# The first weights of experts 4 to 30: four loads of 2 MB for each expert, in place of two of 4 MB

## The chip, the cores and the metric

The kernel runs on one core of one Trainium2 chip. The metric is device time in microseconds (us); of several executions the median counts. A core has TensorE (PE) for matmuls, VectorE (DVE), ScalarE (ACT), GpSimd (POOL), SyncE (SP), which here does nothing but issue loads and stores, and 16 DMA engines that move data between HBM and the on-chip memory (SBUF, 128 partitions).

## The reference

One layer: two token mixers (sparse attention and retention) on 256 tokens of width 1024, and then the part that this document is about, a mixture of 32 experts of which each token uses 4. In float32 throughout:

```python
def moe_ffn(h, w_router, b_router, w1, b1, w2, b2):
    logits = (jnp.einsum('bsd,de->bse', h, w_router) + b_router).astype(jnp.float32)
    top_val, top_idx = lax.top_k(logits, TOP_K)
    ...
    for e in range(N_EXPERTS):
        z = jnp.einsum('bsd,df->bsf', h, w1[e]) + b1[e]
        glu = jnp.minimum(z[..., 0::2], SWIGLU_LIMIT)
        lin = jnp.clip(z[..., 1::2], -SWIGLU_LIMIT, SWIGLU_LIMIT)
        act = glu * jax.nn.sigmoid(SWIGLU_ALPHA * glu) * (lin + 1.0)
        out = out + combine[..., e:e + 1] * (jnp.einsum('bsf,fd->bsd', act, w2[e]) + b2[e])
    return out
```

The first weights w1[e] are 1024 x 2048 numbers (8 MB), the second weights w2[e] 1024 x 1024 (4 MB): 12 MB for an expert and 384 MB in all, every byte read once.

## The kernel before

After the mixers and the router (the first 170 us), the kernel goes through the experts in one sweep, gathering up to 64 tokens for each. On PE one expert is one `step`: eight calls of `z_rows`, each with four matmuls on one row of 2048 numbers of w1 in each partition, and in between smaller pieces (gather and transposes for the next expert, the scatter of results); at its end `down` multiplies the activations of the expert before, e - 1, with its w2, also in eight rows (`k`), four on each half of w2.

Where the weights lie: `w1r` has 16 rows of 128 x 2048 numbers (16 MB), that is room for the w1 of two experts, rows 0 to 7 for even ones and 8 to 15 for odd ones (`par`); `w2r` has room for one w2 (4 MB) in two halves. `w1_used` counts finished rows of w1, `w2_used` finished quarters of w2, both incremented by PE.

SP issues all loads of weights from one queue, in an order that is written out by hand. `load_w2(e, c)` loads half a w2, 2 MB, with runs of 16 KB in each partition. `load_w1(e, i, pair)` loads a quarter of a w1, 2 MB and two rows; it is used for experts 0 to 3 and 31. Experts 4 to 30 go by `next_half(base, e, par, h)`: SP waits until four rows are used, then loads half a w1, 4 MB and four rows, with runs of 32 KB. `next_w2(base, e)` waits for each half of w2 and loads it. `ahead(e, x, par)` is w2 of expert e and then w1 of expert x; `between` puts w2 behind the first half of w1. The loop `Fori(3, 6)` uses `between`, the loop `Fori(6, 15)` uses `ahead`. At the end come the quarters of expert 31 (`next_w1`), the w2 of expert 29 (`next_w2`), and in `last_w2` the w2 of 30 and 31, which go into freed rows of `w1r`; the last one is cut finer still.

PE waits for w1 at the first row of each part: for a half on `w1_half` at rows 0 and 4, for a quarter on `w1_in` at rows 0, 2, 4 and 6. `final` is the last step, with expert 31; the results are normalised and stored behind it.

Of the kernel before, what the change touches and what calls it, by code (L numbers as in the profile page):

```python
# [21 lines left out]
P = 128  # L22
# [7 lines left out]
TOPK_KEYS = 64  # L30
NE, TOPK, FF = 32, 4, 1024
SLOTS = 64
HALVES = 14
SWEEPS = S // SLOTS
KW = P + S
RMS_EPS, LN_EPS = 1e-5, 1e-6
# [38 lines left out]
def hybrid_block(nc, x, norm1_gain, w_in, rel_bias, idx_k_ln_gain, idx_k_ln_bias, ret_gn_gain, w_out,  # L75
# [3 lines left out]
    with ctx:  # L79
        def sb(name, shape, dt=F32):  # L80
            return ctx.enter_context(nc.sbuf_tensor(name, shape, dt))

        def sem(name):
            return ctx.enter_context(nc.semaphore(name))


        w1r = sb("w1r", [P, 16, 2048])
# [127 lines left out]
        dve_chain = sem("dve_chain")  # L215
        w1_in = [sem(f"w1_in{i}") for i in range(8)]
        w2_in = [sem(f"w2_in{i}") for i in range(2)]
        w1_half = [sem(f"w1_half{i}") for i in range(4)]
        w1_early = sem("w1_early")
        w2_last = [sem(f"w2_last{i}") for i in range(6)]  # L220
        w1_used = sem("w1_used"); w2_used = sem("w2_used")
# [11 lines left out]
        x_v = x[0].rearrange("(t p) d -> p t d", p=P)  # L233
        win_v = w_in[0].rearrange("(k p) n -> p k n", p=P)
        w1_v = w_mlp1[0].rearrange("e (c p i a) f -> e c i p (a f)", c=2, p=P, i=2)
        w1_c = w_mlp1[0].rearrange("e (c p j) f -> e c p (j f)", c=2, p=P)
        w2_v = w_mlp2[0].rearrange("e (c p j) d -> e c p (j d)", c=2, p=P)

        C_QI, C_QKB, C_VB, C_GB, C_QA, C_KA, C_VA = range(7)
# [4 lines left out]
        def _(sp):  # L244
# [51 lines left out]
            sp.wait_ge(out_mm, 4)  # L296
            load_w1(1, 0, 4)

            def next_half(base, e, par, h):
                sp.wait_ge(w1_used, 8 * base + (8 * (e - 2) + 4 * h + 4))  # L300
                at = 8 * par + 4 * h
                sp.dma_start(w1r[:, at:at + 4, :].rearrange("p a f -> p (a f)"), w1_c[e, h]).then_inc(w1_half[2 * par + h], 16)

            def next_w1(base, e, par, pairs=range(4)):
                for i in pairs:
                    sp.wait_ge(w1_used, 8 * base + (8 * (e - 2) + 2 * i + 2))
# [20 lines left out]
            def rest_of_sweep(base):  # L327

                def ahead(e, x, par):
                    next_w2(base, e)  # L330
                    next_half(base, x, par, 0)
                    next_half(base, x, par, 1)

                def between(e, x, par):
                    next_half(base, x, par, 0)
                    next_w2(base, e)
                    next_half(base, x, par, 1)

                sp.wait_ge(w1_used, 8 * base + 1)
                sp.dma_start(w1r[:, 0, :], w1_v[2, 0, 0, :, 0:2048]).then_inc(w1_early, 16)  # L340
                sp.wait_ge(w1_used, 8 * base + 2)
                sp.dma_start(w1r[:, 1, :], w1_v[2, 0, 0, :, 2048:4096]).then_inc(w1_in[0], 16)
                next_w1(base, 2, 0, range(1, 4))
                next_w1(base, 3, 1)
                ahead(1, 4, 0)
                ahead(2, 5, 1)
                ahead(3, 6, 0)
                next_w2(base, 4)
                with sp.Fori(3, 6) as m:
                    between(2 * m - 1, 2 * m + 1, 1)  # L350
                    between(2 * m, 2 * m + 2, 0)
                with sp.Fori(6, NE // 2 - 1) as m:
                    ahead(2 * m - 1, 2 * m + 1, 1)
                    ahead(2 * m, 2 * m + 2, 0)
                next_w1(base, NE - 1, 1)
                next_w2(base, NE - 3)
                last_w2(base)
# [4 lines left out]
            with sp.If(n > 1):  # L362
                with sp.Fori(1, n) as r:
                    base = sp.snap(r * NE)
# [678 lines left out]
        def _(pe):  # L1043
# [57 lines left out]
            halves = (slice(0, 64), slice(64, 128))  # L1101
# [28 lines left out]
            for which in range(2):  # L1130
                for g in range(2):
                    for t in range(TT):
                        at = 256 * which + 128 * g
# [27 lines left out]
            for b in range(2):  # L1161
                for j in range(4):
                    k, t = 2 * b + j // 2, j % 2
# [148 lines left out]
                    ins = nc.tensor.transpose(ps[:, 7, P * j:P * j + P], hg[:, P * j:P * j + P], ident)  # L1312
                ins.then_inc(hg_tr, 1)

            def z_rows(base, lap, k, par, halves, early=None):

                if halves and k % 4 == 0:
                    pe.wait_ge(w1_half[2 * par + k // 4], 16 * lap)
                if not halves and k % 2 == 0:
                    pe.wait_ge(w1_in[4 * par + k // 2], 16 * lap)  # L1320
                if early is not None:
                    pe.wait_ge(w1_early, 16 * early)
                for n in range(2):
                    for c in range(2):
                        at = 1024 * c + 512 * n
                        ins = mm(ps[64 * c:64 * c + 64, 2 * par + n, :], hgT[:, par, k % 4, 64 * (k // 4):64 * (k // 4) + 64],  # L1326
                                 w1r[:, 8 * par + k, at:at + 512], start=False, stop=(k == 7))
                ins.then_inc(w1_used, 1)
# [92 lines left out]

            def step(base, hb, wb, rb, m, par, first=False, last=False):
                e = 2 * m + par
                halves = not (isinstance(m, int) and m < 2)
                if halves:
                    lap = rb * (HALVES - par) + m - 1
                else:
                    lap = rb * (2 + par) + m + 1
                head = first and par == 0
                pe.wait_ge(hgT_sb, base + e + 1)  # L1430
                if not (first and par == 0 and isinstance(base, int)):
                    z_bias(base, e, par, free=not first)
                z_rows(base, lap, 0, par, halves, early=rb + 1 if isinstance(m, int) and (m, par) == (1, 0) else None)
                z_rows(base, lap, 1, par, halves)
                if par == 0 and not first:
                    pe.wait_ge(gT_sb, hb + m)
                gather(base, e + 1, 1 - par)
                z_rows(base, lap, 2, par, halves)
                if par == 1 and not first:
                    scatter(base, hb, m - 1, 0)  # L1440
                z_rows(base, lap, 3, par, halves)
                gather_T(base, e + 1)
                z_rows(base, lap, 4, par, halves)
                if par == 1 and not first:
                    scatter(base, hb, m - 1, 1)
                z_rows(base, lap, 5, par, halves)
                if not head:
                    act_T(base, e - 1)
                z_rows(base, lap, 6, par, halves)
                if par == 1:  # L1450
                    gates_T(base, hb, m)
                z_rows(base, lap, 7, par, halves)
                if not head and not last:
                    if par == 1 and not first:
                        pe.wait_ge(added[1], hb + m)
                    if first and isinstance(base, int):
                        pe.wait_ge(first_copied, 2)
                    down(base, wb, e - 1, 1 - par, free=not (first and par == 1))

            def final(base, hb, wb, rb):  # L1460

                e, lap = NE - 1, rb * 3 + 3
                pe.wait_ge(hgT_sb, base + e + 1)
                z_bias(base, e, 1)
                for k in range(4):
                    z_rows(base, lap, k, 1, False)
                pe.wait_ge(z_read, base + e)
                open_sum(0)
                for k in range(4, 7):
                    z_rows(base, lap, k, 1, False)  # L1470
                gates_T(base, hb, NE // 2 - 1)
                z_rows(base, lap, 7, 1, False)
                down(base, wb, e - 2, 1)
                act_T(base, e - 1)
                pe.wait_ge(z_read, base + e + 1)
                open_sum(1)
                pe.wait_ge(actT_sb, base + e)
                act_T(base, e, lin_last)
                pe.wait_ge(based, 2 * rb + 1)
                pe.wait_ge(y_sb, base + e - 1)  # L1480
                pe.wait_ge(y_dve, 3 * rb + 1)
                add_pair(0)
                pe.wait_ge(based, 2 * rb + 2)
                add_pair(1)
                down_late(0, 0, actT, range(8), {0: 0, 4: 1}, hb)
                pe.wait_ge(actT_sb, base + e + 1)
                down_late(1, 4, actT_last, range(4), {0: 2}, hb, bank=6)
                pe.wait_ge(gT_sb, hb + NE // 2)
                pe.wait_ge(y_sb, base + e)
                pe.wait_ge(y_dve, 3 * rb + 2)  # L1490
                for t in range(TT):
                    add_expert(t, 0, gT_last)
                down_late(1, 4, actT_last, range(4, 8), {4: 3, 6: 4, 7: 5}, hb, bank=6)
                pe.wait_ge(y_sb, base + e + 1)
                pe.wait_ge(y_dve, 3 * rb + 3)
                add_expert(0, 1, gT_last, stop=True).then_inc(part_sum, 1)
                add_expert(1, 1, gT_last, stop=True).then_inc(scattered, 4)
# [47 lines left out]
```

## Time and profile before

| | us |
|---|---|
| time, median of 3 runs (1087.14 to 1087.70) | 1087.22 |
| time of the profiled execution | 1086.36 |
| its span, first to last instruction | 1084.6 |
| PE busy in it | 1038.4 |
| of it matmuls on w1 (line 1326) | 487.7 |
| of it matmuls on w2 (line 1352) | 211.8 |
| DVE, ACT and POOL busy | 302.7, 157.0, 22.2 |

A busy time is the time in which an engine had an instruction in work, so a busy PE is not PE at its peak. The page cuts the span into 40 equal slices of 27 us and gives for each the busy share in tenths; for the DMA it gives the mean share of the 16 engines and the GB/s that they moved. Of a DMA the trace has the time at which SP issued it and the time from there to its landing, which holds the time that it stood in the queue behind others. The chain of waits is followed back from the last instruction, at each step to what released it.

### The profile page before, as it was taken

The numbers are of one execution on the slowest core, as the hardware profiler recorded it, in microseconds if no ns is written. First come the engines' busy times: TensorE is split into PE (matmuls) and PEld (weight loads), VectorE is DVE, ScalarE is ACT, GpSimd is POOL, SyncE is SP. The second block draws the span as 40 slices with busy tenths as digits, with TensorE's granted clock in tenths as the row PEclk, the third lists the DMA queues.
The fourth block names the chain that finished last, engine by engine and source line by source line (L and its number), as shares of the span: only waits on it lengthen the run. The fifth ranks groups of instructions, "written<-read, shape, count | busy, mean of one in ns | idle before, by whom it ended". The sixth has DMA issues, their size and how long they took to land.

```text
span 1084.6 us, 11586 instructions
## 1 busy us (share of the span) xinstructions
PE 1038.4 (96%) x4616; PEld 397.4 (37%) x4616; DVE 302.7 (28%) x705; ACT 157.0 (14%) x281; POOL 22.2 (2%) x29
## 2 busy tenths in 40 slices
PE   9999999999999999899999999898989898999996
PEld 7458454333333333233332323232323232333332
DVE  2455623322222223122221312221223222221221
ACT  1231333110101111101010111011111101011111
POOL 1212000000000000000000000000000000000000
PEclk9999999999999999999998999999999999899999
DMA  9886946999999999999999999999999999999995
GB/s 328 238 252 264 387 161 242 429 431 432 432 426 431 433 430 429 431 433 429 429 431 433 428 430 432 425 432 430 431 433 431 433 431 428 430 433 431 424 428 208
DMA packets 34343, 429.75 MB, mean 396 GB/s; under 512 B 5036, under 2 KB 6480, under 8 KB 16496
## 3 DMA queue, kind: packets, MB, share of 16 engines
q1 hardware_dynamic: 32400, 426.03, 93.2%
q10 hardware_dynamic: 1216, 1.70, 1.1%
q0 software_dynamic: 704, 1.71, 0.6%
q8 instruction: 15, 0.25, 0.1%
q14 instruction: 8, 0.07, 0.0%
HBM read 426.80 MB, written 2.62 MB: 396 GB/s over the span
## 4 chain that ended last, share of the span: by engine, by line
PE 67%; DMA 31%; DVE 1%; SPq 1%; issue 0%; ACT 0%; DVEq 0%
PE ps L1326 28%; DMA w1r<-w_mlp 22%; PE ps L1352 13%; DMA w2r<-w_mlp 6%; PE ps L1393 5%; PE ps L1076 4%; PE ps L1304 3%; PE ps L1064 3%; DMA w1r<-w_out 1%; PE ps L1123 1%; PE ps L1229 1%; PE ps L1366 1%; PE ps L1198 1%; DMA w1r<-w_in 1%; PE ps L1334 1%; PE ps L1312 1%
## 5 line engine op out<-in xcount | busy, mean ns | idle before, releaser
L1326 PE MATMUL ps<-w1r,arena 128*64 128x512 f32 x2048 | 487.7, 612 | 28.0 <-DMA w1r<-w_mlp 27.2
L1326 PEld LDWEIGHTS ps<-w1r,arena 128*64 128x64 f32 x2048 | 139.2, 139 | 295.7 <-issue 257.5
L1352 PE MATMUL ps<-w2r,arena 128*64 128x512 f32 x960 | 211.8, 593 | 4.5 <-DMA w2r<-w_mlp 4.5
L1352 PEld LDWEIGHTS ps<-w2r,arena 128*64 128x64 f32 x960 | 68.7, 137 | 142.8 <-issue 135.3
L950 DVE TENSOR_TENSOR acc<-ps,acc 128x512 f32<-128x512 f32 x56 | 36.1, 686 | 180.5 <-PE ps L1393 180.5
L942 DVE TENSOR_TENSOR arena<-arena 128x512 f32<-128x512 f32 x32 | 22.2, 692 | 157.5 <-ACT arena L571 157.4
L575 ACT ACTIVATE arena<-ps 128x512 f32<-128x512 f32 x32 | 19.1, 597 | 289.0 <-PE ps L1334 289.0
L914 DVE TENSOR_TENSOR arena<-ps,cols 128x512 f32<-128x512 f32 x32 | 22.1, 692 | 137.6 <-PE ps L1312 135.9
L1304 PE MATMUL ps<-h,arena 128*64 128x512 f32 x248 | 58.5, 592 | 0.0
L1393 PE MATMUL ps<-arena 128*128 128x512 f32 x112 | 55.5, 618 | 0.0
L580 ACT ACTIVATE arena<-ps 64x512 f32<-64x512 f32 x29 | 17.1, 591 | 263.8 <-PE ps L1352 263.8
L925 DVE TENSOR_SCALAR arena<-small,rank,gate 128x64 f32<-128x64 f32 x128 | 31.3, 308 | 58.1 <-PE ps L1419 58.1
L1076 PE MATMUL ps<-h,w1r 128*128 128x256 f32 x192 | 42.1, 380 | 0.9 <-DMA w1r<-w_in 0.9
L565 ACT ACTIVATE arena<-ps 128x512 f32<-128x512 f32 x31 | 18.5, 597 | 161.1 <-PE ps L1304 161.1
L1076 PEld LDWEIGHTS ps<-h,w1r 128*128 128x128 f32 x192 | 36.2, 190 | 5.9 <-issue 0.9
L936 DVE TENSOR_SCALAR arena<-ps 128x512 f32<-128x512 f32 x32 | 33.6, 1051 | 13.8 <-PE ps L1326 13.8
L905 DVE TENSOR_SCALAR sel_z<-small 96x64 bf16 (+1 forms) x30 | 5.7, 191 | 107.7 <-PE ps L1326 107.7
L937 DVE TENSOR_SCALAR arena<-ps 128x512 f32<-128x512 f32 x32 | 33.9, 1061 | 0.0
L1393 PEld LDWEIGHTS ps<-arena 128*128 128x128 f32 x112 | 19.0, 189 | 36.0 <-issue 36.0
L1304 PEld LDWEIGHTS ps<-h,arena 128*64 128x64 f32 x248 | 17.7, 137 | 35.8 <-issue 35.8
L1064 PE MATMUL ps<-w1r,h 128*128 128x512 f32 x64 | 27.8, 592 | 0.0
L1334 PEld LDWEIGHTS ps<-small,arena 128*128 128x128 f32 x128 | 13.4, 140 | 25.9 <-issue 25.2
(252 smaller groups left out, 575.4 us busy)
## 6 DMA issues: line engine op xcount, KB each, us to landing
w1r<-w_mlp SPq DMA_DIRECT2D x54, 4096.0 KB, 32.0
w2r<-w_mlp SPq DMA_DIRECT2D x60, 2048.0 KB, 18.9
w1r<-w_mlp SPq DMA_DIRECT2D x22, 2048.0 KB, 10.6
w1r<-w_in SPq DMA_DIRECT2D x7, 2048.0 KB, 17.3
w1r<-w_out SPq DMA_DIRECT2D x2, 2048.0 KB, 13.7
w1r<-w_mlp SPq DMA_DIRECT2D x3, 1024.0 KB, 7.3
rel_table<-arena ACTq DMA_DIRECT2D x1, 1536.0 KB
acc<-x SPq DMA_DIRECT2D x2, 512.0 KB, 4.6
```

The costliest lines, as they stand in the source:

```text
L925: ins = v.tensor_scalar(gated[:, t, which, at:at + 64], slotn, rank[:, t, bass.ds(e, 1)], gate[:, t, bass.ds(e, 1)], ALU.is_equal, ALU.mult)
L936: v.tensor_scalar(g3, z[:, :, :, 0], 7.0, None, ALU.min).then_inc(glu_ready, 1)
L937: v.tensor_scalar(l3, z[:, :, :, 1], 7.0, -7.0, ALU.min, ALU.max).then_inc(z_read, 1)
L942: v.tensor_tensor(lin, lin, sig, ALU.mult).then_inc(act_ready, 1)
L950: ins = v.tensor_tensor(sl, ps[:, 4 + c, :], sl, ALU.add)
L1064: ins = mm(ps[:, bank + t, 0:n], hT[:, k, P * t:P * t + P], w[:, k, 0:n], start=(k == 0), stop=(k == KD - 1))
L1076: ins = mm(ps[:, bank + g // 2, S * (g % 2):S * (g % 2) + S], w[:, k, P * g:P * g + P], hT[:, k, :], start=(k == 0), stop=(k == KD - 1))
L1304: ins = mm(ps[64 * c:64 * c + 64, 6, :], onehotP[:, par, t, :], h2[:, t, :].rearrange("p (j c q) -> p c j q", j=4, c=2)[:, c], start=(t == ...
L1326: ins = mm(ps[64 * c:64 * c + 64, 2 * par + n, :], hgT[:, par, k % 4, 64 * (k // 4):64 * (k // 4) + 64], w1r[:, 8 * par + k, at:at + 512], ...
L1334: ins = nc.tensor.transpose(ps[:, 7, P * j:P * j + P], lin[:, P * j:P * j + P], ident)
L1352: ins = mm(ps[at:at + 64, 4 + c, :], actT[:, k % 4, 64 * (k // 4):64 * (k // 4) + 64], w2r[:, k // 2, col:col + 512], start=(k == 0), stop ...
L1393: ins = mm(ps[:, 4 + c, :], gT[:, c, P * t:P * t + P], ysb[:, c, :], start=not with_bias, stop=True)
```

## The change

`next_half` is gone, and with it the view `w1_c`, the four semaphores `w1_half`, and the constant HALVES. Experts 4 to 30 are loaded by `next_w1`, as 2, 3 and 31 were: four quarters of 2 MB, each behind its own wait for two rows. PE waits on `w1_in` at rows 0, 2, 4 and 6 of every expert. The bytes and the buffers are the same.

```diff
-            def next_half(base, e, par, h):
-                sp.wait_ge(w1_used, 8 * base + (8 * (e - 2) + 4 * h + 4))
-                at = 8 * par + 4 * h
-                sp.dma_start(w1r[:, at:at + 4, :].rearrange("p a f -> p (a f)"), w1_c[e, h]).then_inc(w1_half[2 * par + h], 16)
-
                 def ahead(e, x, par):
                     next_w2(base, e)
-                    next_half(base, x, par, 0)
-                    next_half(base, x, par, 1)
+                    next_w1(base, x, par)
 
                 def between(e, x, par):
-                    next_half(base, x, par, 0)
+                    next_w1(base, x, par, range(2))
                     next_w2(base, e)
-                    next_half(base, x, par, 1)
+                    next_w1(base, x, par, range(2, 4))
...
-            def z_rows(base, lap, k, par, halves, early=None):
-
-                if halves and k % 4 == 0:
-                    pe.wait_ge(w1_half[2 * par + k // 4], 16 * lap)
-                if not halves and k % 2 == 0:
+            def z_rows(base, lap, k, par, early=None):
+
+                if k % 2 == 0:
                     pe.wait_ge(w1_in[4 * par + k // 2], 16 * lap)
```

The two views of w1 in HBM are

```python
w1_v = w_mlp1[0].rearrange("e (c p i a) f -> e c i p (a f)", c=2, p=P, i=2)
w1_c = w_mlp1[0].rearrange("e (c p j) f -> e c p (j f)", c=2, p=P)
```

A half by `w1_c` is 4 MB without a gap, four rows of w1 (32 KB) for each partition. A quarter by `w1_v` takes two of these four rows, a run of 16 KB every 32 KB; the other two come with the next quarter.

SP's queue, first half of the body of the loop `Fori(6, 15)` before. A DMA of 128x8192 is 4 MB, one of 128x4096 is 2 MB; an ISA row is the wait:

```order
L352 ISA
L254 ISA [waits w2_used]
L254 DMA w2r<-w_mlp 128x4096
L311 REGISTER_ALU
L254 ISA [waits w2_used]
L254 DMA w2r<-w_mlp 128x4096
L300 ISA
L302 ISA [waits w1_used]
L302 DMA w1r<-w_mlp 128x8192
L300 REGISTER_ALU
L302 ISA [waits w1_used]
L302 DMA w1r<-w_mlp 128x8192
```

The same place after the change, from the second wait for w2 on:

```order
L251 ISA [waits w2_used]
L251 DMA w2r<-w_mlp 128x4096
L298 ISA
L248 ISA [waits w1_used]
L248 DMA w1r<-w_mlp 128x4096
L298 REGISTER_ALU
L248 ISA [waits w1_used]
L248 DMA w1r<-w_mlp 128x4096
```

Two more such pairs follow: four waits and loads stand where two stood; rows of w1 keep their order, and the w2 ahead of them stays where it was.

PE, the first rows of an odd expert in the loop, before (`w1_half2` is the first half of an odd expert, `w1_half3` the second):

```order
L1326 MATMUL ps<-w1r,arena 64x512 [waits w1_half2]
L1326 MATMUL ps<-w1r,arena 64x512 x7
L1304 MATMUL ps<-h,arena 64x512 [waits p_ready]
L1304 MATMUL ps<-h,arena 64x512 x3
L1326 MATMUL ps<-w1r,arena 64x512 x4
```

And after, where `w1_in4` and `w1_in5` are its first two quarters:

```order
L1315 MATMUL ps<-w1r,arena 64x512 [waits w1_in4]
L1315 MATMUL ps<-w1r,arena 64x512 x7
L1295 MATMUL ps<-h,arena 64x512 [waits p_ready]
L1295 MATMUL ps<-h,arena 64x512 x3
L1315 MATMUL ps<-w1r,arena 64x512 [waits w1_in5]
L1315 MATMUL ps<-w1r,arena 64x512 x3
```

The matmuls stand in the same order; the first wait asks for 2 MB in place of 4, and there is one more before the third row.

## Rows read from the trace of the kernel before

**Rows 1.** The page: span, then DMA busy tenths and GB/s in 40 slices
```profile
span 1084.6 us, 11586 instructions
...
DMA  9886946999999999999999999999999999999995
GB/s 328 238 252 264 387 161 242 429 431 432 432 426 431 433 430 429 431 433 429 429 431 433 428 430 432 425 432 430 431 433 431 433 431 428 430 433 431 424 428 208
```

**Rows 2.** The page's DMA issues: count, KB each, median us to landing
```profile
w1r<-w_mlp SPq DMA_DIRECT2D x54, 4096.0 KB, 32.0
w2r<-w_mlp SPq DMA_DIRECT2D x60, 2048.0 KB, 18.9
```

**Rows 3.** Waits of PE for DMAs, whole span: us in total, times, longest
```profile
PE ps L1326 <- DMA w1r<-w_mlp: 27.2, 12, 4.4
PE ps L1352 <- DMA w2r<-w_mlp: 4.5, 4, 1.6
```

**Rows 4.** Windows: engines' busy us (x), then PE clock, DMA share, GB/s
```profile
188.00:250.00 62.00, 62.00 (x300) 21.06 (x296) 14.99 (x31) 8.00 (x14) 0.00 (x0) 1.00 1.01 429
600.00:980.00 380.00, 360.10 (x1600) 120.75 (x1596) 87.62 (x180) 43.45 (x74) 0.00 (x0) 0.97 1.00 431
```

**Rows 5.** Chain of waits at experts 19 and 29: start us, us, what
```profile
661.69 27.00 DMA w1r<-w_mlp
...
688.74 5.35 PE ps L1326 x16
...
955.06 25.80 DMA w1r<-w_mlp
...
980.90 3.65 PE ps L1326 x16
```

**Rows 6.** Timeline of PE, last part: start us, us, instructions, wait
```profile
1019.83 3.65 PE L1326 MATMUL ps<-w1r,arena 128*64 128x512 f32 x16 [0.32 <-DMA w1r<-w_mlp]
...
1049.18 3.65 PE L1352 MATMUL ps<-w2r,arena 128*64 128x512 f32 x16 [1.14 <-DMA w2r<-w_mlp]
...
1058.17 10.52 PE L1366 MATMUL ps<-w1r,arena 128*64 128x512 f32 x48
...
1070.54 3.65 PE L1366 MATMUL ps<-w1r,arena 128*64 128x512 f32 x16
```

**Rows 7.** Two loads of 2 MB, w1 of expert 3, w2: issue, landing
```profile
L251 SPq DMA_DIRECT2D w1r<-w_mlp x1: 328/328/328, 199.8 to 199.8; - x1
DMA to landing us min/median/max: 11.0/11.0/11.0
...
L254 SPq DMA_DIRECT2D w2r<-w_mlp x1: 328/328/328, 215.7 to 215.7; - x1
DMA to landing us min/median/max: 14.7/14.7/14.7
```

**Rows 8.** Chain of waits, the same place two experts apart: start us, us
```profile
341.83 6.87 PE ps L1352 x32
...
395.16 6.87 PE ps L1352 x32
```

**Rows 9.** Timeline of SP: the closest issues, early and in the loop
```profile
224.77 8.67 SPq L302 DMA_DIRECT2D w1r<-w_mlp  x2
...
657.65 3.75 SPq L254 DMA_DIRECT2D w2r<-w_mlp  x2
```

**Rows 10.** Timeline of SP at the end: issues that took long
```profile
1028.07 1.49 SPq L324 DMA_DIRECT2D w1r<-w_mlp  x1
1029.60 4.24 SPq L325 DMA_DIRECT2D w1r<-w_mlp  x1
```

**Rows 11.** Timeline of PE: matmuls behind the longest wait
```profile
571.89 6.07 PE L1326 MATMUL ps<-w1r,arena 128*64 128x512 f32 x16 [4.37 <-DMA w1r<-w_mlp]
```

**Rows 12.** A load of 1 MB into an idle queue: issue, landing
```profile
L340 SPq DMA_DIRECT2D w1r<-w_mlp x1: 328/328/328, 175.8 to 175.8; - x1
DMA to landing us min/median/max: 4.8/4.8/4.8
```

More of the change, by code:

```diff
@@ L32 @@
 SLOTS = 64
-HALVES = 14
 SWEEPS = S // SLOTS
@@ L217, in hybrid_block @@
         w2_in = [sem(f"w2_in{i}") for i in range(2)]
-        w1_half = [sem(f"w1_half{i}") for i in range(4)]
         w1_early = sem("w1_early")
@@ L235, in hybrid_block @@
         w1_v = w_mlp1[0].rearrange("e (c p i a) f -> e c i p (a f)", c=2, p=P, i=2)
-        w1_c = w_mlp1[0].rearrange("e (c p j) f -> e c p (j f)", c=2, p=P)
         w2_v = w_mlp2[0].rearrange("e (c p j) d -> e c p (j d)", c=2, p=P)
@@ L1423, in step @@
                 e = 2 * m + par
[L1424 to L1428, printed above, removed]
+                lap = rb * (NE // 2) + m + 1
                 head = first and par == 0
@@ L1432, in step @@
                     z_bias(base, e, par, free=not first)
-                z_rows(base, lap, 0, par, halves, early=rb + 1 if isinstance(m, int) and (m, par) == (1, 0) else None)
-                z_rows(base, lap, 1, par, halves)
+                z_rows(base, lap, 0, par, early=rb + 1 if isinstance(m, int) and (m, par) == (1, 0) else None)
+                z_rows(base, lap, 1, par)
                 if par == 0 and not first:
@@ L1437, in step @@
                 gather(base, e + 1, 1 - par)
-                z_rows(base, lap, 2, par, halves)
+                z_rows(base, lap, 2, par)
                 if par == 1 and not first:
                     scatter(base, hb, m - 1, 0)
-                z_rows(base, lap, 3, par, halves)
+                z_rows(base, lap, 3, par)
                 gather_T(base, e + 1)
-                z_rows(base, lap, 4, par, halves)
+                z_rows(base, lap, 4, par)
                 if par == 1 and not first:
                     scatter(base, hb, m - 1, 1)
-                z_rows(base, lap, 5, par, halves)
+                z_rows(base, lap, 5, par)
                 if not head:
                     act_T(base, e - 1)
-                z_rows(base, lap, 6, par, halves)
+                z_rows(base, lap, 6, par)
                 if par == 1:
                     gates_T(base, hb, m)
-                z_rows(base, lap, 7, par, halves)
+                z_rows(base, lap, 7, par)
                 if not head and not last:
@@ L1460, in final @@
             def final(base, hb, wb, rb):
-                e, lap = NE - 1, rb * 3 + 3
+                e, lap = NE - 1, (rb + 1) * (NE // 2)
                 pe.wait_ge(hgT_sb, base + e + 1)
@@ L1465, in final @@
                 for k in range(4):
-                    z_rows(base, lap, k, 1, False)
+                    z_rows(base, lap, k, 1)
                 pe.wait_ge(z_read, base + e)
@@ L1469, in final @@
                 for k in range(4, 7):
-                    z_rows(base, lap, k, 1, False)
+                    z_rows(base, lap, k, 1)
                 gates_T(base, hb, NE // 2 - 1)
-                z_rows(base, lap, 7, 1, False)
+                z_rows(base, lap, 7, 1)
                 down(base, wb, e - 2, 1)
```

## The prediction

> **What bounds the kernel now.** I read the slices of the page first. From the eighth slice on (190 us) the DMA row shows a 9 in every slice but the last, and the GB/s row stays between 424 and 433 whatever the experts do [rows 1]. Finer windows say the same: a DMA share of 1.01 from 188 to 250 us and of 1.00 from 600 to 980 us [rows 4]. PE looks just as busy, but it waits: 12 times for w1 and 4 times for w2, together 31.7 us [rows 3], and the chain of waits passes through a load at each of the waits in the loop [rows 5]. Which of the two sets the pace is told by two periods. While PE still had weights in store, the same place of the program came back after 395.16 - 341.83 = 53.33 us, two experts [rows 8]; that is PE's own pace. From the wait at 688.74 to the one at 980.90 us, five such periods later, it is (980.90 - 688.74)/5 = 58.43 us [rows 5]. In 58.43 us the queue moves the 24 MB of two experts (25.17 million bytes), 430.7 GB/s, which is the rate of the window. So the stream of weights is the bound from about 190 us to its last landing, and PE has 5.1 us to spare in every two experts. The end hangs on it as well: PE takes up w2 of expert 29 at 1049.18 us, behind a wait of 1.14 us for its landing [rows 6], and what follows is 1084.6 - 1049.2 = 35.4 us of work with no long wait. The time is therefore the start of the stream, plus its bytes at its rate, plus 35.4 us.
>
> **Moving the waits, at no cost.** SP's order of bytes is the same before and after; a quarter is asked for after two used rows in place of four, so no load is issued later. Does any issue come too late for a full queue? The closest one in the loop is the w2 at 657.65 us [rows 9]. The half of w1 that lands at 661.69 + 27.00 = 688.69 us [rows 5] has two parts of w2 (4.89 us each, below) ahead of it, and the queue before those ends at 688.69 - 9.72 - 2 x 4.89 = 669.2 us, 11.5 us after the issue. Early on the closest is the first half for expert 4, issued at 224.77 us [rows 9] while the w2 ahead of it lands at 215.7 + 14.7 = 230.4 us [rows 7], 5.6 us later. The DMA row hides nothing that earlier issues could fill. PE may start a step up to 4.9 us sooner, on the first quarter, and the waits of rows 3 will be spread over more and shorter ones. That moves PE closer to the stream, and PE's place doesn't matter: the last wait of importance is for w2 of expert 29, which has four quarters of expert 31 ahead of it in the queue, and these are 2 MB already. I count nothing for it, and nothing for the two more waits of SP and PE for each half (each an instruction beside a queue that is full, and PE has its 5.1 us).
>
> **The rate, which is the whole cost.** What is left is whether 4 MB take the same time as one load with runs of 32 KB and as two with runs of 16 KB. The trace has both kinds. Between the release of PE at 1019.83 us (second half of expert 30) and the one at 1049.18 us (second part of w2 of expert 29) the queue served four quarters of expert 31 and two parts of w2 [rows 6], six loads of 2 MB with runs of 16 KB: 29.35/6 = 4.892 us each. A period of two experts holds four loads of 4 MB and four of 2 MB, so one of each takes 58.43/4 = 14.608 us, and the 4 MB alone 14.608 - 4.892 = 9.716 us. Two quarters take 9.784 us. The change costs 0.068 us for each half, and there are 54 halves [rows 2]: 3.7 us. Nothing hides it, since the stream is the bound all the while.
>
> How firm is 0.068? It is a small difference of large terms, so I look for bounds. Early quarters of w1, which have the very form of the new ones (16 KB out of every 32 KB), give an upper one: from the landing at 199.8 + 11.0 = 210.8 us to that at 230.4 us [rows 7] lie two of them and two parts of w2, 19.6/4 = 4.90 us each; with the rounding of the two rows, 4.87 to 4.93. At 4.90 the sum is 54 x (9.80 - 9.716) = 4.5 us; at the ends it is 1.3 us and 7.8 us. The windows are coarser: 429 GB/s where nearly all is 2 MB, against 431 in the loop [rows 4]; an expert at 429 throughout takes 29.33 us and not 29.22, which over 27 experts is 3.1 us. I take 3.7, since its rows have hundredths over six loads and over five periods. It also fits what a run costs: a load is 128 runs, 8 for each of the 16 engines, and 0.068 us for 8 more runs on each is 8.5 ns a run.
>
> The Trainium skill, "DMA: Bandwidth & Descriptors", section "Measured (HBM→SBUF, 128 partitions, SWDGE, issued from GpSimd)", has about 10.5 ns for a packet as the floor of small transfers. As an estimate by that page, 8 more runs would be 0.084 us and the whole change 54 x 0.084 = 4.5 us, 0.8 us above mine, and inside the range of the early quarters.
>
> Sum: the profiled execution of 1086.36 us (span 1084.6) becomes 1090.0 us, and the median, which lies 0.9 us above it, 1087.22 + 3.7 = **1090.9 us**.
>
> **The rivals.**
> *No change (1087.2 us).* The 0.068 us would be an accident of the end, where quarters of expert 31 and the last w2 flow, or a part of it would be a cost of the turn from one kind of load to the other, which goes away when all are alike. For it: the difference is 0.7% of a load and comes from one stretch of six. Against it: the early stretch, at 429 GB/s and 4.90 us, says the same [rows 4, 7]. It decides if the new loads take under 4.88 us.
>
> *Faster.* The waits were for 4 MB and are now for 2 MB; if a wait of PE set the end, the first quarter would be there 4.9 us sooner, and the time would be 1087.2 + 3.7 - 4.9 = 1086.0 us; if every wait on w1 counted it would be 27.2 us less [rows 3]. Against it: the 1.14 us before the end are waited for w2, behind quarters that don't change [rows 6], and a stream at share 1.00 can't be sped up by asking earlier.
>
> *Much slower, by the clock.* Behind the wait of 4.37 us at 571.89 us, 16 matmuls took 6.07 us, where 3.65 are usual [rows 11, 6]. Stops cost PE up to 2.4 us beyond their length. With quarters PE stops more often: if each of four stops in a step, eight in two experts, cost that much, it would be 19 us in place of the 5.1 us to spare, 14 us more for two experts, about 98 us over the seven periods from 571 to 981 us: 1189 us. It decides when PE's work in two experts passes 58.4 us. Against it: a quarter needs 3.6 us of matmuls and comes every 4.9 us, so the stops would be of 1.3 us, and the one of 1.14 us at the end was followed by 3.65 us, full speed [rows 6].
>
> *Much slower, by a start-up cost of each load.* A load of 1 MB into an idle queue landed after 4.8 us [rows 12], where 1.05 million bytes at 431 GB/s are 2.4 us. If every one of the 54 additional loads paid 2.4 us, the time would be 1087.2 + 130 = 1217 us. Against it: the queued loads of 2 MB follow each other after 4.892 us, at 429 GB/s, so the next one moves while the last one lands. The Trainium skill, same page, section "Anatomy of one DMA — SWDGE (gpsimd) path", has this as a fixed 2.0 us for each DMA; by that rule alone it would be an estimated 108 us. The trace disagrees for loads that stand in a full queue.
>
> *A full queue on SP.* At the end SP's issues took 1.49 and 4.24 us in place of 0.33 [rows 10]: there are so many loads under way then that SP has to wait for one to land. With quarters there are more under way, so this will be seen more often. I price it at nothing: SP then stands still because the queue is full, so the DMA engines have work, and behind the waiting issue are only further loads.
>
> **How the numbers follow.** A cost of 2 MB runs in the range 1.3 to 6 us: 0.88, and in it over 0.2% (2.2 us, about the least that a measurement of this kernel can tell from no change) 0.82. No change, and a cost under 2.2 us: together 0.12. Faster: 0.04. The two much slower ones, and what I haven't seen: 0.02 together, on the slower side, which makes 0.84. The range runs from 1088.8 (a cost of 1.6 us) to 1092.8 us (5.6 us); it leaves out the faster case, most of no change, the far end of the early rows and the last two.
>
> **What would show it.** Landings every 4.89 us all through the loop, a period of 58.7 us for two experts in place of 58.43, GB/s of 429 where 431 stood, PE's waits for w1 more in number and none above 3 us, PE's last wait for w2 at about 1052.9 us and 35.4 us behind it. I am wrong if the period stays at 58.43 (the runs of 16 KB cost nothing here), if the DMA share falls under 1.00 anywhere in the loop (the queue ran dry), or if the stretch behind the last wait changes its length.

## The result

| | before | after |
|---|---|---|
| median of six runs of each, us | 1087.70 | 1091.93 |
| ratio, 95% interval | | 1.0034 (1.0021 to 1.0047) |
| profiled execution, its span, us | 1086.36, 1084.6 | 1090.92, 1089.1 |
| PE busy, us | 1038.4 | 1033.4 |
| two experts in the loop, us | 58.43 | 58.73 |

The change made the kernel slower by 0.34%: 3.7 us by the ratio (2.3 to 5.1), 4.2 us between the two medians. 3.7 us and a median of 1090.9 us were predicted; 1091.93 us came. The page of the changed kernel, with the lines that answer to [rows 1] and [rows 2] (span, DMA in 40 slices; then issues by count, KB and median us to landing):

```profile
span 1089.1 us, 11784 instructions
...
DMA  9886946999999999999999999999999999999994
GB/s 332 233 251 270 377 159 258 431 427 428 428 426 430 427 429 428 428 428 428 428 429 428 428 428 429 428 429 428 430 427 430 427 430 427 430 427 430 427 428 194
...
w1r<-w_mlp SPq DMA_DIRECT2D x130, 2048.0 KB, 30.4
w2r<-w_mlp SPq DMA_DIRECT2D x60, 2048.0 KB, 23.5
```

The DMA row is as full as before, and the GB/s row stands mostly at 427 to 430, where it stood mostly at 429 to 433. The windows answer to [rows 4] (busy us of PE, PEld, DVE, ACT and POOL, then PE clock, DMA share, GB/s):

```profile
188.00:250.00 62.00, 62.00 (x300) 21.05 (x298) 15.23 (x32) 8.00 (x14) 0.00 (x0) 1.00 1.01 427
600.00:980.00 380.00, 349.36 (x1574) 114.77 (x1572) 86.98 (x180) 41.70 (x71) 0.00 (x0) 1.00 1.01 428
```

The loop moved from 431 to 428 GB/s at a full share. PE got better and it did not help: it is busy for 349.36 us of these 380, before for 360.10, and its clock is 1.00 where it was 0.97. Its waits, against [rows 3] (us in total, times, longest):

```profile
PE ps L1341 <- DMA w2r<-w_mlp: 22.2, 17, 3.1
PE ps L1315 <- DMA w1r<-w_mlp: 18.4, 28, 1.2
```

There are 45 waits in place of 16, none for w1 is longer than 1.2 us where the longest was 4.4, and the sum rose from 31.7 to 40.6 us: PE finishes its work sooner and waits the rest away. The period, from the chain of waits as in [rows 5] (start us, us, what):

```profile
598.24 29.01 DMA w1r<-w_mlp
...
627.29 3.65 PE ps L1315 x16
...
950.63 28.99 DMA w1r<-w_mlp
...
979.67 3.65 PE ps L1315 x16
```

(979.67 - 627.29)/6 = 58.73 us, six periods. And the end, against [rows 6], from PE's timeline:

```profile
1053.06 3.65 PE L1341 MATMUL ps<-w2r,arena 128*64 128x512 f32 x16 [1.14 <-DMA w2r<-w_mlp]
...
1062.05 10.52 PE L1355 MATMUL ps<-w1r,arena 128*64 128x512 f32 x48
...
1074.41 3.65 PE L1355 MATMUL ps<-w1r,arena 128*64 128x512 f32 x16
```

The wait for w2 of expert 29 is 1.14 us as before and ends 3.88 us later (1053.06 against 1049.18). Everything up to 1074.41 us is 3.87 us later, and so is the issue of the last store, by SP; the remaining 0.6 us of the span came in this one issue, which took 1.74 us and not 1.09. Before, and after:

```profile
1080.71 1.09 SPq L377 DMA_DIRECT2D out<-w1r  x1
```

```profile
1084.58 1.74 SPq L368 DMA_DIRECT2D out<-w1r  x1
```

### The profile page after: what moved, and what is told of

Its sections match the earlier page's. It is cut to its first block, busy times and chain, and to the rows that moved or that the text cites. A ratio compares the mean times of both kernels' runs of the same rounds, so it can differ in the third digit from the quotient of the medians.

```text
span 1089.1 us, 11784 instructions
## 1 busy us (share of the span) xinstructions
PE 1033.4 (95%) x4616; PEld 393.3 (36%) x4616; DVE 302.5 (28%) x705; ACT 157.0 (14%) x281; POOL 22.2 (2%) x29
## 4 chain that ended last, share of the span: by engine, by line
PE 68%; DMA 30%; DVE 1%; SPq 1%; issue 0%; ACT 0%; DVEq 0%
PE ps L1315 28%; DMA w1r<-w_mlp 21%; PE ps L1341 14%; DMA w2r<-w_mlp 6%; PE ps L1382 5%; PE ps L1067 4%; PE ps L1295 3%; PE ps L1055 3%; DMA w1r<-w_out 1%; PE ps L1114 1%; PE ps L1220 1%; PE ps L1355 1%; PE ps L1189 1%; PE ps L1323 1%; PE ps L1303 1%; DMA w1r<-w_in 1%
## 5 line engine op out<-in xcount | busy, mean ns | idle before, releaser
L1315 PE MATMUL ps<-w1r,arena 128*64 128x512 f32 x2048 | 474.9, 598 | 19.7 <-DMA w1r<-w_mlp 18.4
L1341 PE MATMUL ps<-w2r,arena 128*64 128x512 f32 x960 | 216.2, 600 | 22.2 <-DMA w2r<-w_mlp 22.2
L1315 PEld LDWEIGHTS ps<-w1r,arena 128*64 128x64 f32 x2048 | 135.5, 136 | 280.8 <-issue 237.7
L1295 PE MATMUL ps<-h,arena 128*64 128x512 f32 x248 | 58.5, 592 | 0.0
L1295 PEld LDWEIGHTS ps<-h,arena 128*64 128x64 f32 x248 | 17.8, 137 | 35.4 <-issue 35.4
```

What stands on the lines that cost most here:

```text
L1295: ins = mm(ps[64 * c:64 * c + 64, 6, :], onehotP[:, par, t, :], h2[:, t, :].rearrange("p (j c q) -> p c j q", j=4, c=2)[:, c], start=(t == ...
L1341: ins = mm(ps[at:at + 64, 4 + c, :], actT[:, k % 4, 64 * (k // 4):64 * (k // 4) + 64], w2r[:, k // 2, col:col + 512], start=(k == 0), stop ...
```

## The experiments

All ratios below are to the kernel before, with both run on the same chip. The period is the time of two experts in the loop, read as above. Of the cuts of code, `...` marks what is left out.

### Is it the length of a run, the number of loads, or the gaps in HBM?

The change alters three things at once: runs of 16 KB for 32, twice as many loads, and in HBM 16 KB out of every 32 KB in place of a solid block. Three kernels take one each, a fourth doubles the dose.

**Loads of 4 MB with runs of 16 KB.** PE's order of rows is adapted (`d` in place of `k` for the activations).

```diff
-        w1_c = w_mlp1[0].rearrange("e (c p j) f -> e c p (j f)", c=2, p=P)
+        w1_c = w_mlp1[0].rearrange("e (c p i a) f -> e i p c (a f)", c=2, p=P, i=2)
...
-                sp.dma_start(w1r[:, at:at + 4, :].rearrange("p a f -> p (a f)"), w1_c[e, h])...
+                sp.dma_start(w1r[:, at:at + 4, :].rearrange("p (c a) f -> p c (a f)", c=2), w1_c[e, h])...
```

> The kernel before, with its 54 loads of 4 MB and its waits, but each load takes a run of 16 KB from each half of w1 for a partition, so 256 runs of 16 KB in place of 128 of 32 KB. The same sums, in another order of rows. Theory of the run (each run costs 8 to 9 ns more on its engine, whatever the size of the load): a period of two experts of 58.7 us, and 3.7 to 4.2 us more than before (ratio 1.0034 to 1.0039). Rival, a cost of each load: nothing changes, 58.43 us and ratio 1.000.

Measured: 1092.33 us median, ratio 1.0051 (1.0025 to 1.0077). The chain of waits:

```profile
546.15 28.99 DMA w1r<-w_mlp
...
633.87 0.04 issue
...
959.96 26.28 DMA w1r<-w_mlp
```

From the landing at 546.15 + 28.99 = 575.14 us to that at 959.96 + 26.28 = 986.24 us are seven periods of 58.73 us; the line in between begins at a landing one period after the first, 633.87 us. The ratio is above the expected 1.0034 to 1.0039, but its interval holds them. This is the changed kernel's period, at the number of loads and with the waits of the kernel before. The number of loads costs nothing that shows; the run does. The waits of PE are not it either: they are the old ones here.

**Loads of 2 MB with runs of 32 KB**, cut by partitions.

```diff
-                sp.dma_start(w1r[:, at:at + 4, :]..., w1_c[e, h]).then_inc(w1_half[2 * par + h], 16)
+                for q in range(2):
+                    sp.dma_start(w1r[64 * q:64 * q + 64, at:at + 4, :]..., w1_c[e, h][64 * q:64 * q + 64]).then_inc(w1_half[2 * par + h], 16)
```

> The kernel before with each load of 4 MB cut in two of 2 MB by partitions (0 to 63, 64 to 127), so the runs stay at 32 KB and the number of loads is that of the changed kernel. Theory of the run: period 58.43 us, ratio 1.000 to 1.001. Rival, a cost of each load: period 58.7 us, ratio 1.0034. If half the partitions take loads at a lower rate, both are wrong and it is far slower.

Measured: 1848.67 us, ratio 1.6914 (1.6838 to 1.6991). The third case of the expectation came true and the test says nothing on the number of loads. What it shows by its windows is another thing:

```profile
350.00:550.00 200.00, 133.27 (x510) 41.91 (x508) 29.06 (x59) 13.00 (x22) 0.00 (x0) 0.82 1.00 242
```

In this stretch the DMA engines are busy all the time (share 1.00), at 242 GB/s, just over half the rate. A third of these bytes is w2, on 128 partitions; the loads on 64 partitions, 2 MB each, land about 9.9 us apart (at 433.2, 443.1 and 452.9 us), where 2 MB on 128 take 4.89. A busy share is no rate.

**Quarters that are solid in HBM.** This kernel multiplies rows of w1 with the wrong activations, and is for its time alone.

```diff
+        w1_q = w_mlp1[0].rearrange("e (q p a) f -> e q p (a f)", q=4, p=P)
...
-                ..., w1_v[e, i // 2, i % 2]).then_inc(w1_in[pair], 16)
+                ..., w1_q[e, i]).then_inc(w1_in[pair], 16)
```

> The changed kernel, but each quarter of w1 is 2 MB without a gap in HBM (runs of 16 KB one behind the other), where the changed kernel takes 16 KB out of every 32 KB. Rows of w1 then meet other activations than they should; the work is the same in kind and amount. Theory of the run: as the changed kernel, period 58.73 us and ratio 1.0034 to 1.0041 to the kernel before. Rival, the gaps in HBM cost it: period back at 58.43 us and ratio 1.000.

Measured: 1092.03 us, ratio 1.0039 (1.0025 to 1.0053). Its chain of waits:

```profile
600.75 29.05 DMA w1r<-w_mlp
...
953.22 28.99 DMA w1r<-w_mlp
```

(982.21 - 629.80)/6 = 58.74 us. The gaps in HBM cost nothing; a solid block of 2 MB in runs of 16 KB is as slow.

**Runs of 8 KB**, in the 108 loads of the changed kernel.

```diff
+        w1_s = w_mlp1[0].rearrange("e (c p i a) f -> e c a p i f", c=2, p=P, i=2)
...
+                        sp.dma_start(w1r[:, at:at + 2, :], w1_s[e, i // 2, i % 2]).then_inc(w1_in[4 * par + i], 16)
```

> The changed kernel with runs of 8 KB for experts 4 to 30 (a quarter holds every second row of its half, in the same 108 loads). The same sums in another order of rows. Theory of the run: 8 more runs per engine in each quarter, 0.068 to 0.074 us, so 8 x 0.07 = 0.56 us on a period, 59.3 us, and 108 x 0.07 = 7.6 us on top of the changed kernel, 11.3 to 12 us over the kernel before (ratio 1.0105 to 1.011). Rival, a cost of each load: as the changed kernel, 58.73 us, ratio 1.0034 to 1.004.

Measured: 1099.59 us, ratio 1.0117 (1.0095 to 1.014).

```profile
602.45 29.61 DMA w1r<-w_mlp
...
958.53 29.64 DMA w1r<-w_mlp
...
600.00:980.00 380.00, 347.08 (x1564) 114.07 (x1562) 87.03 (x180) 41.99 (x71) 0.00 (x0) 1.00 1.01 424
```

(988.17 - 632.06)/6 = 59.35 us a period, at 424 GB/s and a full share. The dose counts: from 32 to 16 KB a load of 4 MB became (58.73 - 58.43)/4 = 0.074 us longer, 9.3 ns for each of the 8 runs more on an engine; from 16 to 8 KB a load of 2 MB became (59.35 - 58.73)/8 = 0.078 us longer, 9.7 ns a run. The total rose by 1.17%, a little more than the 1.05 to 1.1% expected, which its interval holds. The Trainium skill, "DMA: Bandwidth & Descriptors", section "Measured (HBM→SBUF, 128 partitions, SWDGE, issued from GpSimd)", has about 10.5 ns for a packet of a small transfer. The 9.3 and 9.7 ns of these loads of 2 and 4 MB, which SP issues, come near it.

The other way round, the longer run for w2, was tried next.

### Is the stream the bound, and how far is PE from it?

**12 and 24 more transposes on PE for each expert**, in the changed kernel; the first is

```diff
-                for j in range(4):
+                for j in list(range(4)) * 4:
```

in `gather_T`, the second has 7 in place of 4.

> The changed kernel with 12 transposes more on PE in each expert, 1.8 us, 3.6 us in two experts (each transpose of the gathered tokens is made four times). If the stream of weights is the bound, PE's own pace becomes about 57 us and stays under the period: 58.73 us and a total within 1 us of the changed kernel (ratio 1.0034 to 1.005 to the kernel before). If PE counts, 31 x 1.8 = 56 us more.

> The same with 24 transposes more in each expert, 3.6 us, 7.1 us in two: PE's own pace becomes 60.4 us, over the period of 58.73. The stream theory says that PE is now the bound: period about 60.4 us, DMA share under 1.00 in the loop, and the total 15 to 35 us over the changed kernel. This is the other side of the 5.4 us that PE has to spare.

Measured: 1096.40 us, ratio 1.0074 (1.0058 to 1.009), and 1120.96 us in one run. The first was to stay within 1 us of the changed kernel and came out 4.5 us slower. The second came out 29 us slower, inside the 15 to 35 us expected, but not for the reason given: its period did not rise to 60.4 us and its DMA share did not fall in the loop (1.01 at 429 GB/s from 600 to 980 us). First, how much was added, from the groups of PE (line, engine, op, count | busy us, mean ns | idle), the kernel before, then the two:

```profile
L1312 PE MATMUL ps<-small,arena 128*128 128x128 f32 x124 | 20.4, 287 | 0.0
```

```profile
L1303 PE MATMUL ps<-small,arena 128*128 128x128 f32 x496 | 61.0, 276 | 0.0
```

```profile
L1303 PE MATMUL ps<-small,arena 128*128 128x128 f32 x868 | 101.6, 275 | 0.0
```

So 40.6 us and 81.2 us in all, 1.3 and 2.6 us an expert and not 1.8 and 3.6. PE's own pace in the second is 53.33 + 2 x 2.6 = 58.5 us, just under the stream's 58.73, and the trace has 58.56 (the same 32 matmuls on w2 start at 568.74 and at 627.30 us); PE ran there without a single wait for a DMA. The case of a PE clearly slower than the stream was thus not reached. Second, what it cost. The first took 40.6 us more on PE and was 4.5 us slower than the changed kernel (medians), so PE is not the bound, but it is not without effect either. From 600 to 980 us the first keeps the changed kernel's rate, 428 GB/s at a share of 1.01; the time was lost before. The timeline of SP shows where, the changed kernel and then this one:

```profile
461.86 0.91 SPq L248 DMA_DIRECT2D w1r<-w_mlp  x2
486.95 3.75 SPq L251 DMA_DIRECT2D w2r<-w_mlp  x2
```

```profile
470.83 0.91 SPq L248 DMA_DIRECT2D w1r<-w_mlp  x2
497.23 3.75 SPq L251 DMA_DIRECT2D w2r<-w_mlp  x2
```

Here the order changes from `between` to `ahead`: the first half of the next w1, which `between` would ask for in the middle of a step, now comes behind w2. For about 25 us SP asks for nothing. In the changed kernel the load before lands 32.7 us after its issue at 462.4 us, at 495.1 us, 8.1 us behind SP's next issue. With more work on PE the last one is issued at 471.4 us and lands after 27.4 us, at 498.8 us, only 1.6 us behind the next issue at 497.23 us; the queue was empty for a moment, and the following load landed 1.5 us late. Windows of this place, with 0, 12 and 24 transposes more:

```profile
480.00:520.00 40.00, 40.00 (x196) 13.80 (x192) 10.40 (x23) 5.30 (x9) 0.00 (x0) 1.00 1.01 429
```

```profile
480.00:520.00 40.00, 40.00 (x200) 15.58 (x198) 9.76 (x25) 4.20 (x7) 0.00 (x0) 1.00 0.99 414
```

```profile
480.00:520.00 40.00, 40.00 (x196) 15.41 (x194) 10.71 (x20) 5.31 (x9) 0.00 (x0) 1.00 0.80 331
```

The stream of the first is 5.9 us late at its end. Beside this stop, 1.1 us were there at 230 us, 0.8 of them before the loads of weights at 176 us, and so no stop of the stream; 3.1 us came where the order changes for the first time. There the w2 was issued 0.17 us behind the end of the queue, at 329.24 us, and landed 3.2 us late:

```profile
329.40 3.77 SPq L251 DMA_DIRECT2D w2r<-w_mlp  x2
```

With 24 transposes the issues at these two places came 4.0 and 5.2 us behind the end of the queue, and the landings 7.0 and 8.3 us late. That is half of its 29 us; another 6.6 us are a longer end behind the last landing of w2r. PE's place matters once an issue comes too close to the end of the queue, and that is at the changes of order first. How close can be read off: between 300 and 1000 us, in the traces of all kernels here whose loads take 128 partitions, every issue 4.0 us or more ahead of the queue's end left no gap, apart from a few late landings with 25 us and more still queued, and all 13 that came 3.6 us ahead or less did leave one, from 0.2 us upward.

### A longer run for w2

**w2 as one load of 4 MB with runs of 32 KB.** The rows of w2 that a partition holds must then lie together, so PE takes the columns of w1 in another order.

```diff
-        w2_v = w_mlp2[0].rearrange("e (c p j) d -> e c p (j d)", c=2, p=P)
+        w2_v = w_mlp2[0].rearrange("e (p c j) d -> e c p (j d)", c=2, p=P)
+        w2_w = w_mlp2[0].rearrange("e (p j) d -> e p (j d)", p=P)
...
-                for c in range(2):
-                    sp.wait_ge(w2_used, 4 * base + (4 * (e - 1) + 2 * c + 2))
-                    load_w2(e, c)
+                sp.wait_ge(w2_used, 4 * base + 4 * e)
+                load_w2(e)
...
+            def columns(row, n, c):
+                return row[:, 1024 * n:1024 * n + 1024].rearrange("p (q c r) -> p c q r", c=2, r=8)[:, c]
```

> The kernel before, but w2 of an expert comes as one load of 4 MB with runs of 32 KB in place of two of 2 MB with runs of 16 KB (experts 0 to 29; PE waits for the whole of it). For that, PE reads the columns of w1 in another order. Theory of the run (9 ns a run): 0.07 us less for each w2, so a period of 58.29 us, and 29 x 0.07 = 2.0 us less in all, ratio 0.998, faster than both kernels. Rivals: w2 asked for later makes the queue run dry (the period grows over 58.43 us), or PE is slowed by the order of columns, which the control without the larger load would show too.

> Control for the one with w2 in 4 MB: the same order of columns on PE, but w2 still in two loads of 2 MB with runs of 16 KB, now out of every 32 KB. Theory of the run: as the kernel before, period 58.43 us and ratio 1.000. If the order of columns costs PE time, its matmuls on w1 take over 612 ns in the mean, and the period still stays, as long as PE has work for under 58.4 us.

Measured: with 4 MB 1096.19 us, ratio 1.0072 (1.0058 to 1.0086); the control 1087.57 us, ratio 0.9996 (0.9985 to 1.0007), period (980.69 - 630.07)/6 = 58.44 us, 612 ns a matmul on w1: the order of columns is free. The period with 4 MB:

```profile
604.54 28.56 DMA w1r<-w_mlp
...
955.91 26.86 DMA w1r<-w_mlp
```

(982.77 - 633.10)/6 = 58.28 us, as expected; against the control that is 9.9 ns a run. And yet it is slower by 8 us. Its windows and its end on PE:

```profile
480.00:520.00 40.00, 40.00 (x192) 13.76 (x192) 11.01 (x24) 5.51 (x10) 0.00 (x0) 1.00 0.93 395
600.00:980.00 380.00, 357.73 (x1598) 118.98 (x1596) 87.82 (x181) 42.02 (x71) 0.00 (x0) 0.98 1.00 432
...
1052.55 9.89 PE L1352 MATMUL ps<-w2r,arena 128*64 128x512 f32 x32 [5.42 <-DMA w2r<-w_mlp]
```

The whole w2 is asked for only when its second half could be, 3.4 us behind the first in the kernel before, and the queue stops at the changes of order, by 1.0 us near 339 and 2.7 us near 507 us. At the end PE waits 5.42 us for the whole of w2, and needs 1094.6 - 1052.4 = 42.2 us from there, where 35.4 were enough.

**The parts of 2 MB back at the ends** (w2 of experts 0 and 29), then with other orders in the loops. The edit of the second loop for `between` in both:

```diff
                 with sp.Fori(6, NE // 2 - 1) as m:
-                    ahead(2 * m - 1, 2 * m + 1, 1)
-                    ahead(2 * m, 2 * m + 2, 0)
+                    between(2 * m - 1, 2 * m + 1, 1)
+                    between(2 * m, 2 * m + 2, 0)
```

> The one with w2 in single loads of 4 MB, but w2 of experts 0 and 29 in two parts of 2 MB again. In the other, PE took 42.2 us behind the landing of w2 of expert 29, since it could do neither half before; the kernel before takes 35.4. Expected: period 58.28 us still, 35.5 us behind the last w2, so 6.8 us less than that one, ratio about 1.001 to the kernel before. What is left over a ratio of 0.998 are stops of the queue, 1.0 us near 330 us and 2.7 us near 500 us. If the end stays at 42 us, the reading of the end is wrong.

> The same with the order of the first loop (half of w1, w2, half of w1) kept in the second loop, so that no change of order leaves the queue without work near 500 us. Expected: the 2.7 us there go, period 58.28 us, ratio 0.9985 to 0.999 to the kernel before. Rival: w2 now stands behind 4 MB more, PE waits for it, and the end moves later by what PE lacks; then the ratio is over 1.001.

> The same, and in the first loop both halves of w1 ahead of w2, so that the stop of 1.0 us near 330 us goes too. Expected: ratio 0.9975 to 0.998, the full 2 us of the longer runs. Rival: w2 behind both halves comes too late for PE, which then asks too late in its turn: a stop of another kind, ratio 1.000 or more.

> Control: the kernel before, w2 in two parts of 2 MB, with the order of the first loop kept in the second. The stream of the kernel before has no stop to remove, so by the stream theory period 58.43 us and ratio 1.000; if this alone is faster, what the ones with 4 MB gain is not from their runs.

| | median, us | ratio (95%) | PE's wait for w2, us, times |
|---|---|---|---|
| parts at the ends | 1089.56 | 1.0022 (1.0013 to 1.0031) | 14.0, 13 |
| and `between` in both loops | 1091.84 | 1.0039 (1.0026 to 1.0052) | 34.3, 12 |
| and both halves of w1 ahead of w2 in the first | 1094.12 | 1.0065 (1.0048 to 1.0082) | 35.7, 11 |
| the kernel before with `between` in both | 1088.70 | 1.0015 (1.0006 to 1.0024) | 33.4, 13 |

The reading of the end holds: with the parts the wait is 1.16 us again, at 1053.11 us, and 36.0 us follow.

```profile
480.00:520.00 40.00, 40.00 (x190) 13.85 (x190) 11.01 (x24) 4.82 (x9) 0.00 (x0) 1.00 0.91 386
...
1053.11 3.65 PE L1363 MATMUL ps<-w2r,arena 128*64 128x512 f32 x16 [1.16 <-DMA w2r<-w_mlp]
```

The stops stay, 2.7 us near 341 us and 1.6 us near 507 us, and they and a late landing of 1.7 us near 1029 us, for which I have no cause, are more than the 2 us gained. The other orders failed by the rival of their expectation: with `between` in both loops the stop near 500 us goes, with both halves of w1 ahead in the first loop the one near 330 us (and one of 1.6 us near 504 us comes). The period stays 58.28 us, but w2 stands behind more of w1, PE waits for w2 in nearly every period, and reaches the end late: with `between` in both, 41 us of work follow the last landing of w2r (1050.3 us, span 1091.3 us). The last row shows that cost on its own: the same order in the kernel before is 0.15% slower, where no difference was expected; its last w2 lands when it did, at 1049.1 us, and 36.3 us follow in place of 35.5. No version beat the kernel before.

## Why the prediction was right

*The bound.* Right. The stream was full before and after (share 1.00 and 1.01), and neither PE's better clock nor 10.7 us less of PE time in the window of 380 us bought anything. The step that PE's place does not matter holds for this change, since PE moved forward. It is too strong as written: with PE moved back by 1.3 us an expert the time rose by 4.5 us. I had named as the closest issues one 5.6 us ahead early and one 11.5 us ahead in the loop. In the trace before the closest ones were others: 5.5 us at 264.33 us, 7.0 us at 321.23 us and 9.4 us at 484.52 us. The last two are the changes of order, near 330 and 490 us, and those are the places that stop first.

*The waits at no cost.* Right. The last wait stayed at 1.14 us. What follows it took 36.0 us and not 35.4, which I had named as a sign of being wrong; the work of PE in it is the same (21.36 and 21.35 us to its last matmuls on w1r), and the 0.6 us are the one longer issue of the last store, so the sign does not speak against the mechanism. In the kernel with loads of 4 MB and runs of 16 KB the old waits go with the new period, so they are no part of the loss.

*The rate.* Right, a little small: 0.074 us for each half and not 0.068, 54 x 0.074 = 4.0 us and not 3.7. Of the two traces, the stream's last wait moved by 3.88 us, and the stream came up to expert 4 0.3 us earlier in the changed kernel (a landing at 230.10 in place of 230.44 us), so that its bytes took 4.2 us more. The kernel's ratio gives 3.7 us (2.3 to 5.1); that it meets the forecast to the tenth is luck. The estimate by early quarters (4.5 us) was too high, the one by windows (3.1 us) too low; the early window, said to be nearly all loads of 2 MB, held two of 4 MB, about 20 of its 62 us. The form of the cost, so much for a run and nothing for a load, was an assumption of the prediction; the experiments on 4 MB in runs of 16 KB and on runs of 8 KB show it.

*The rivals.* The accident of the end is out, as the solid quarters and the ones of 4 MB show the same period. The faster case is out: the end did not hang on a wait for w1. The clock went the other way. In the kernel before PE stopped for w1 once in two experts, for 2.0 to 4.4 us, eight times from 571 us on, and with seven of these stops (all but the one of 2.0 us) the granted clock was at its lower level, 1.2 GHz, for 3.4 or 6.8 us. Two rows of one such stop, the second a window (busy us, then clock, DMA share, GB/s), and the same window after:

```profile
747.18 5.35 PE L1326 MATMUL ps<-w1r,arena 128*64 128x512 f32 x16 [3.20 <-DMA w1r<-w_mlp]
...
746.00:754.00 8.00, 6.82 (x24) 2.18 (x26) 0.11 (x1) 0.00 (x0) 0.00 (x0) 0.79 1.00 430
```

```profile
746.00:754.00 8.00, 8.00 (x34) 2.60 (x32) 0.28 (x2) 0.60 (x1) 0.00 (x0) 1.00 1.02 432
```

In the changed kernel no stop from 560 to 980 us is over 1.3 us, and the clock stays at its upper level; it fell once between 180 and 1080 us, for 6.8 us, at the stop of 3.1 us for w2 at 451 us. The start-up cost of a load doesn't show in a full queue: 54 loads more cost nothing beside their runs. SP did stand still at the end, for 10.7 us, and it cost nothing:

```profile
1028.25 10.71 SPq L317 DMA_DIRECT2D w1r<-w_mlp  x1
```

*What was to be seen.* A period of 58.7 us, GB/s of 429 and a last wait at 1052.9 us were named; 58.73, 428 and 1053.06 came. For w1 more waits were named, none above 3 us; 28 came, the longest of 1.2 us. The longest wait of all, 3.1 us, was for w2.

## What to carry to other kernels

When the DMA share is 1.00 and the engines wait in turn, price a change of loads, as long as they go to all 128 partitions, by the length of their runs: here 9 to 10 ns for each run on an engine, at 2 and at 4 MB a load alike, hidden by nothing. Get the two rates from the trace by timing known sequences of loads between two waits, since slices and windows are too coarse for a difference of 0.7%. And before a load is made larger, look at two places: where the order of issues changes (how far ahead of the end of the queue does the next issue come? 4 us were enough here) and the last wait (what could begin on the first part?); the gain of 2 us from longer runs for w2 was lost at both.

## What the runs showed of the hardware

A load on 64 of the 128 partitions runs at half the rate: 2 MB in 9.9 us against 4.89 on 128, with the DMA engines busy at share 1.00 in both, and the kernel took 1.69 times as long. It seems to be the number of runs that fills SP's queue, and not the number of loads: with runs of 8 KB four issues of 2 MB took SP 14.13 us, 11.39 of them in the last one, where with 16 KB they take 2.08 us. That last load lands 42.3 us after its issue in both, so as much work stood ahead of it. The landings stayed without a gap, and it cost nothing.

```profile
572.26 14.13 SPq L302 DMA_DIRECT2D w1r<-w_mlp  x4
```

```profile
568.55 2.08 SPq L248 DMA_DIRECT2D w1r<-w_mlp  x4
```

A clock that falls behind a stop is a sign and not a cost as long as another engine is the bound: from 600 to 980 us PE ran at a mean granted clock of 0.97 before and of 1.00 after, and the slower clock belonged to the faster kernel.
